# A first norm taken token by token on ScalarE, and the first two projections by chunk pairs

## The chip, the cores and the metric

The kernel runs on one core of one Trainium2 chip. The metric is the device time of one execution in microseconds. Five engines work side by side and meet only at semaphores: TensorE (PE; its weight loads are shown as PEld), VectorE (DVE), ScalarE (ACT), GpSimd (POOL) and SyncE (SP), which issues the DMAs.

## The reference, cut to what matters

Two transformer blocks over 512 tokens of width 1024, in float32. The first thing that is computed is a root-mean-square norm of x and the input projection:

```python
def rms_norm(x, g, eps=NORM_EPS):
    x32 = x.astype(jnp.float32)
    y = x32 * lax.rsqrt(jnp.mean(x32 * x32, axis=-1, keepdims=True) + eps)
    return (y * g.astype(jnp.float32)).astype(x.dtype)

h = rms_norm(x, norm_mix_pre_g[l])
proj = h @ w_in[l]
mq, mk, mv, dq, dk, dv, ga, gb = jnp.split(proj, split_at, axis=-1)
```

All that follows (two kinds of attention, gates, output projections, feed-forward parts, a second block with a recurrent mixer, stick-breaking attention and a memory) is the same in both kernels.

## The kernel before, in words

Activations are kept transposed: the width lies on partitions in 8 chunks of 128, the 512 tokens along the free axis. A matmul in full precision is made of three: each weight tile (128 output columns, 8 chunks, 512 KB in DRAM, buffer RAW) is split by `split` into a high part WH (ACT, L1178) and a rest WL (DVE, L1402); each activation chunk X is multiplied by the norm's gain and split into HH (ACT, L1184) and HL (DVE, L1412) by `feed`. `mm` (L971) then issues, for one chunk k and each weight of its group, WH with HH, WL with HH and WH with HL into one PSUM bank: 24 matmuls for a weight.

The norm's factor R per token is not applied before the projections but to their results: `normed` (L1431) multiplies the PSUM bank by R. So matmuls can begin before R is known.

A planner (`Plan`) writes one list of steps; each engine's program walks through that list in order and carries out the steps that it has a part in. The order of the list is therefore the order on every engine, and an engine that waits holds back all that stands behind it. Events are semaphores: `hi`/`lo` for a weight's parts, `xh`/`xl` for a chunk's, `mm` for the end of a projection.

The start of the kernel:

- SP issues the loads: chunk pairs of x (`load_x`, L1829, 512 KB each, tokens on partitions) and the first four weights in turn: x0, w0, x2, w1, x4, w2, x6, w3, then 17 small loads (`small_loads`), then further weights. Weight n goes into one of 4 RAW buffers and waits for the WL of weight n - 4.
- `turn_x` (L950): four 128x128 transposes on TensorE per chunk, into a bank; DVE copies it to X (L1407).
- `turns` (L474) is a generator: for chunk c it emits the transposes and the copy, then the `feed` of chunk c - 1, for c = 0 and 1 also the split of a weight. Three of its steps run before the first projection, the rest one by one in front of each `mm` step. So transposes stand two or three chunks ahead of the matmuls of the first group, q and k of head pair 0, which take both weights chunk by chunk.
- The sum of squares: `feed` calls `square`. ACT squares X per chunk (L1189), POOL adds to an accumulator (L1762), DVE adds the last (L1419), TensorE multiplies it by `onesD` (every element 1/1024, L1005), which gives the mean square of each token on all partitions, and `rstd` makes R of it: a table load (L115), Ln (L1197) and Exp (L1199) on ACT and three 128x512 operations on DVE (L1425, L1427, L1429).

After the group, `split_to` has ACT and DVE split weights 3 and 4 (counted from 0; they wait for the end of the first and second weight's matmuls, whose buffers they take), then come the steps of the norm, and then the third weight, vr.

## Time and profile before

| | us |
|---|---|
| median of 3 runs | 1995.89 |
| lowest, highest | 1995.13, 1997.08 |
| the profiled execution | 1994.75 |
| its span, first to last instruction | 1992.7 |

The page of the profile: PE busy 1962.3 us (98% of the span), PEld 1591.4, DVE 979.6, ACT 760.2, POOL 247.3; mean DMA rate 88 GB/s; mean granted clock of TensorE 0.997 of full speed. Busy times of single matmuls overlap, since they are pipelined; the time that one takes up is the distance from its start to the next one's. Times in the rows are microseconds from the start of the span; "xN" is a number of instructions merged into a row, and what stands in brackets is the idle time of the engine before the row and what ended it.

### The profile page before, as it was taken

Reading aid. Unit: us, or ns where it says so; the run is one execution under the profiler, and the core shown is the slowest. Engines: PE = TensorE matmul, PEld = TensorE weight load, DVE = VectorE, ACT = ScalarE, POOL = GpSimd, SP = SyncE. Lnnn points to the kernel's source line nnn. Section 1 sums busy time; section 2 is a strip of 40 time slices with the busy share of each in tenths; the row PEclk is TensorE's granted clock in tenths of the full one; section 3 lists DMA queues with packets and bytes.
Section 4 is the critical chain, followed back from the end, with each engine's and each line's share of the span. In section 5 each row is a group of like instructions: output and inputs, shape, how many; then the busy total and the mean of one; then the engine's idle time right before and its main releaser. Section 6 shows DMA issues by size and latency. Waiting matters only on the chain.

```text
span 1992.7 us, 22832 instructions
## 1 busy us (share of the span) xinstructions
PE 1962.3 (98%) x9092; PEld 1591.4 (80%) x9092; DVE 979.6 (49%) x1508; ACT 760.2 (38%) x1150; POOL 247.3 (12%) x253
## 2 busy tenths in 40 slices
PE   8999999999999999999999999999999999999997
PEld 6777788878888887788888878877887788888886
DVE  6677534373334335533433465675654454333334
ACT  5344523453232234422322355565543343222233
POOL 5221001201011011110100130122010011011012
PEclk9999999999999999999999999999999999999998
DMA  5212223433333324333333231211231233333322
GB/s 162 85 53 64 64 85 95 117 97 103 98 95 95 96 82 119 90 100 95 96 95 96 89 91 55 64 53 53 85 95 53 85 96 95 95 97 102 98 80 58
DMA packets 343402, 175.71 MB, mean 88 GB/s; under 512 B 6305, under 2 KB 343298, under 8 KB 343298
## 3 DMA queue, kind: packets, MB, share of 16 engines
q1 hardware_dynamic: 343298, 174.27, 30.1%
q8 instruction: 72, 1.18, 0.2%
q14 instruction: 32, 0.26, 0.0%
HBM read 172.15 MB, written 2.10 MB: 87 GB/s over the span
## 4 chain that ended last, share of the span: by engine, by line
PE 89%; DVE 7%; ACT 2%; issue 1%; DMA 0%; SPq 0%; POOL 0%; DVEq 0%; ACTq 0%
PE ps L982 27%; PE ps L986 27%; PE ps L984 27%; DVE WL L1402 1%; PE ps L1022 1%; PE ps L1042 1%; PE ps L1059 1%; PE ps L1120 1%; PE ps L995 1%; PE ps L1138 1%; PE ps L1012 1%; DVE TS L1435 1%; PE ps L1051 1%; DVE TS L1599 1%; PE ps L1063 1%
## 5 line engine op out<-in xcount | busy, mean ns | idle before, releaser
L1402 DVE TENSOR_TENSOR WL<-RAW,WH 128x1024 fp32r<-128x1024 f32 (+2 forms) x336 | 400.9, 1196 | 707.6 <-ACT WH L1178 707.3
L982 PE MATMUL ps<-HH,WH 128*128 128x512 f32 x1728 | 688.0, 398 | 0.0
L986 PE MATMUL ps<-HL,WH 128*128 128x512 f32 x1728 | 674.4, 390 | 2.0 <-DVE HL L1412 1.9
L984 PE MATMUL ps<-HH,WL 128*128 128x512 f32 x1728 | 673.6, 390 | 1.0 <-DVE WL L1402 1.0
L1178 ACT ACTIVATE WH<-RAW 128x1024 fp32r<-128x1024 f32 (+2 forms) x336 | 342.2, 1021 | 546.4 <-PE ps L986 538.1
L982 PEld LDWEIGHTS ps<-HH,WH 128*128 128x128 f32 x1728 | 324.7, 188 | 76.1 <-issue 8.8
L986 PEld LDWEIGHTS ps<-HL,WH 128*128 128x128 f32 x1728 | 324.6, 188 | 73.8 <-DVE HL L1412 5.6
L984 PEld LDWEIGHTS ps<-HH,WL 128*128 128x128 f32 x1728 | 324.8, 188 | 72.7 <-issue 5.3
L982 PE MATMUL ps<-GH,WH 128*128 128x512 f32 x720 | 282.0, 392 | 0.0
L986 PE MATMUL ps<-GL,WH 128*128 128x512 f32 x720 | 280.6, 390 | 0.0
L984 PE MATMUL ps<-GH,WL 128*128 128x512 f32 x720 | 280.2, 389 | 0.0
L1781 POOL TENSOR_TENSOR TS<-TS 128x512 f32<-128x512 f32 x66 | 85.1, 1290 | 936.4 <-ACT TS L1206 936.4
L986 PEld LDWEIGHTS ps<-GL,WH 128*128 128x128 f32 x720 | 135.1, 188 | 29.5 <-DVE GL L1441 1.3
L982 PEld LDWEIGHTS ps<-GH,WH 128*128 128x128 f32 x720 | 135.2, 188 | 28.8 <-ACT GH L1221 0.8
L984 PEld LDWEIGHTS ps<-GH,WL 128*128 128x128 f32 x720 | 135.2, 188 | 28.3 <-issue 0.5
L1206 ACT ACTIVATE TS<-TS 128x512 f32<-128x512 f32 x90 | 56.9, 632 | 212.4 <-DVE TS L1435 212.4
L1435 DVE SCALAR_TENSOR_TENSOR TS<-ps,TS 128x512 f32<-128x512 f32 x142 | 97.2, 686 | 81.2 <-PE ps L986 80.5
L1221 ACT ACTIVATE GH<-TS 128x512 fp32r<-128x512 f32 x78 | 49.3, 632 | 180.8 <-DVE TS L1532 125.0
L1762 POOL TENSOR_TENSOR TS<-TS 128x512 f32<-128x512 f32 (+1 forms) x48 | 60.4, 1258 | 374.6 <-ACT TS L1189 374.4
L1441 DVE TENSOR_TENSOR GL<-TS,GH 128x512 fp32r<-128x512 f32 x78 | 54.0, 692 | 54.5 <-ACT GH L1221 54.5
L1184 ACT ACTIVATE HH<-X,G 128x512 fp32r<-128x512 f32 x48 | 34.7, 723 | 64.0 <-DVE X L1557 44.5
L1412 DVE SCALAR_TENSOR_TENSOR HL<-X,G,HH 128x512 fp32r<-128x512 f32 x48 | 39.4, 822 | 19.3 <-ACT HH L1184 19.0
(197 smaller groups left out, 1509.1 us busy)
## 6 DMA issues: line engine op xcount, KB each, us to landing
RAW<-in_ffn_w_gu SPq DMA_DIRECT2D x88, 512.0 KB, 3.8
RAW<-in_w_in SPq DMA_DIRECT2D x68, 512.0 KB, 3.9
RAW<-in_ffn_w_down SPq DMA_DIRECT2D x32, 512.0 KB, 4.1
RAW<-in_w_gate SPq DMA_DIRECT2D x22, 512.0 KB, 3.7
RAW<-in_w_up SPq DMA_DIRECT2D x22, 512.0 KB, 3.9
RAW<-in_w_out SPq DMA_DIRECT2D x16, 512.0 KB, 4.1
RAW<-in_mem_w_kv SPq DMA_DIRECT2D x16, 512.0 KB, 3.9
RAW<-in_w_down SPq DMA_DIRECT2D x16, 512.0 KB, 4.1
```

The lines of the kernel that those rows point to most:

```text
L982: e.matmul(bk, wh, xh, start=k == 0, stop=False)
L984: e.matmul(bk, wl, xh, start=False, stop=False)
L986: last = e.matmul(bk, wh, xl, start=False, stop=k == kt - 1)
L1178: e.activation(m["WH"][:, s, 0:kt, :], m["RAW"][:, n % NRAW, 0:kt, :], ACT.Copy).then_inc(*sg.inc("hi", n))
L1206: e.activation(t, t, ACT.Silu if func == "Silu" else ACT.Sigmoid).then_inc(*sg.inc("fn", key))
L1221: e.activation(m[buf + "H"][:, n, :], at.view(src), ACT.Copy).then_inc(*sg.inc("xh", (buf, gen, n)))
L1402: e.tensor_tensor(m["WL"][:, s, 0:kt, :], m["RAW"][:, n % NRAW, 0:kt, :], m["WH"][:, s, 0:kt, :].bitcast(F32), ALU.subtract).then_inc(*sg. ...
L1412: e.scalar_tensor_tensor(m["HL"][:, c, :], X[:, c, :], G[:, gcol:gcol + 1], m["HH"][:, c, :].bitcast(F32), ALU.mult, ALU.subtract).then_in ...
L1435: e.scalar_tensor_tensor(at.tile(key), at.bank(bank), scale, at.tile(("R", R)), ALU.mult, ALU.mult).then_inc(*sg.inc("pj", key))
L1441: e.tensor_tensor(m[buf + "L"][:, n, :], at.view(src), m[buf + "H"][:, n, :].bitcast(F32), ALU.subtract).then_inc(*sg.inc("xl", (buf, gen, ...
L1762: e.tensor_tensor(a, a, s, ALU.add).then_inc(*sg.inc("acc", (acc, c)))
L1781: e.tensor_tensor(t, t, at.tile(("R", R)), ALU.mult).then_inc(*sg.inc("gr", key))
```

## The change

It does the following.

- The loads of x4 and x6 go ahead of the third and fourth weight.
- The first two projections are emitted by `first_pair`: for each pair of chunks c, c+1, the transposes and copies of both, the feeds of both, for c = 0 and 2 the split of one weight, the squares of the pair, then matmul steps of that pair for one weight (`which`), then for the other. At c = 0 only the first weight is taken; at c = 2 the second takes k = 0 to 3. After the last pair come the splits of weights 2, 3 and 4.
- The squares are taken on ACT from x as it was loaded (tokens on partitions): per pair four 128x256 activations with an accumulated sum along the row, into the 16 columns of XS. POOL's and DVE's adds of this norm are gone.
- `first_norm` replaces `rstd` for this norm: DVE sums XS to four values per partition and scales them, ACT takes Ln and Exp of 128x4 values, DVE refines them in three 128x4 operations and scales the identity four times into `diag`; TensorE multiplies `onesD` by `diag`, which spreads the four columns over all partitions, and DVE copies the bank to R.
- The scratch for dynamic DMA is 2048 in place of 4096; two small buffers are added.

```diff
+    def turn_pair(self, c):
+        for a in range(2):
+            self.bank(("tx", c + a))
+            self.step("turn_x", c + a)
+            self.banks.give(("tx", c + a), ("x", (0, c + a)))
+        for a in range(2):
+            self.step("feed", 0, c + a, c + a, ())
...
+    def first_pair(self, ps):
+
+        banks = [self.bank(("pb", key)) for key, *_ in ps]
+        self.weights += [(name, 0, KD, c0) for _, name, c0, *_ in ps]
+        self.groups.append((0, 2, ("H", 0, 0), banks, T, KD))
+        for c in range(0, KD, 2):
+            self.turn_pair(c)
+            if c < 4:
+                self.step("split", c // 2)
+            self.square_pair(c)
+            for i in range(2):
+                if (c, i) == (0, 1):
+                    continue
+                for k in range(0 if (c, i) == (2, 1) else c, c + 2):
+                    self.step("mm", 0, k, (i,))
+        self.n_split = 2
+        self.split_to(2 + NSPL)
+        return [self.normed(0, p[0], b, ("mm", i), *p[3:]) for i, (p, b) in enumerate(zip(ps, banks))]
...
@@ run
-            if self.total:
+            if self.total and c < 4:
                 self.dma()
+        for _ in range(2 if self.total else 0):
+            self.dma()
         self.tiles.take("small")
         self.step("small_loads")
-        turn = self.turns()
-        for _ in range(EARLY):
-            next(turn)
-        self.first_block(turn)
+        self.first_block()
...
@@ tensor_program
+    def first_norm(key):
+        g.wait_ge(*sg.at("ones", 0))
+        g.wait_ge(*sg.at("diag", 0))
+        wait_all(at.bank_free(("stat", key)))
+        e.matmul(at.bank(("stat", key)), m["onesD"], at.tile("diag"), start=True, stop=True).then_inc(*sg.inc("stat", key))
...
@@ scalar_program
+    def square_x(c):
+        v = at.x_pair(c)
+        g.wait_ge(*sg.at(f"d_x{c}", c))
+        for j in range(4):
+            h = slice(j % 2 * 256, j % 2 * 256 + 256)
+            wait_all(at.tile_free(("xq", c, j // 2)))
+            o = e.activation(at.tile(("xq", c, j // 2))[:, h], v[:, j, :], ACT.Square, accum_out=m["XS"][:, 4 * j + c // 2:4 * j + c // 2 + 1])
+        o.then_inc(*sg.inc("xq", c))
+
+    def first_norm(key):
+        N = m["XN"]
+        explog()
+        g.wait_ge(*sg.at("xm", 0))
+        g.wait_ge(*sg.at("ones", 0))
+        e.activation(N[:, 4:8], N[:, 0:4], ACT.Ln, bias=m["eps"][:, 0:1], scale=4.0).then_inc(*sg.inc("rs"))
+        g.wait_ge(*sg.last("rs"))
+        e.activation(N[:, 4:8], N[:, 4:8], ACT.Exp, scale=-0.5).then_inc(*sg.inc("rs", key))
...
@@ vector_program
+    def first_norm(key):
+        N, d = m["XN"], at.tile("diag").rearrange("p (i f) -> p i f", f=P)
+        for c in range(0, KD, 2):
+            g.wait_ge(*sg.at("xq", c))
+        e.tensor_reduce(N[:, 8:12], m["XS"].rearrange("p (i c) -> p i c", c=4), AX.X, ALU.add).then_inc(*sg.inc("xn"))
+        g.wait_ge(*sg.last("xn"))
+        e.tensor_scalar(N[:, 0:4], N[:, 8:12], 1.0 / D, None, ALU.mult).then_inc(*sg.inc("xm", 0))
+        g.wait_ge(*sg.at("rs", key))
+        e.scalar_tensor_tensor(N[:, 8:12], N[:, 4:8], 4.0, N[:, 4:8], ALU.mult, ALU.mult).then_inc(*sg.inc("xn"))
+        g.wait_ge(*sg.at("xm", 0))
+        g.wait_ge(*sg.last("xn"))
+        e.scalar_tensor_tensor(N[:, 8:12], N[:, 0:4], 1e-6, N[:, 8:12], ALU.add, ALU.mult).then_inc(*sg.inc("xn"))
+        g.wait_ge(*sg.last("xn"))
+        e.scalar_tensor_tensor(N[:, 4:8], N[:, 8:12], 3.0, N[:, 4:8], ALU.subtract, ALU.mult, reverse0=True).then_inc(*sg.inc("xn"))
+        g.wait_ge(*sg.last("xn"))
+        g.wait_ge(*sg.at("ident", 0))
+        wait_all(at.tile_free("diag"))
+        for j in range(4):
+            o = e.tensor_scalar(d[:, j, :], m["ident"], N[:, 4 + j:5 + j], float(D), ALU.mult, ALU.mult)
+        o.then_inc(*sg.inc("diag", 0))
+        g.wait_ge(*sg.at("stat", key))
+        wait_all(at.tile_free(("R", key)))
+        e.tensor_copy(at.tile(("R", key)), at.bank(("stat", key))).then_inc(*sg.inc("R", key))
...
-    nc = _bacc.Bacc("TRN2", target_bir_lowering=False, num_devices=1, dynamic_dma_scratch_size=4096)
+    nc = _bacc.Bacc("TRN2", target_bir_lowering=False, num_devices=1, dynamic_dma_scratch_size=2048)
```

## Rows read from the trace of the kernel before

**Rows 1.** The page: busy times, and the chain that ended last by engine.

```profile
PE 1962.3 (98%) x9092; PEld 1591.4 (80%) x9092; DVE 979.6 (49%) x1508; ACT 760.2 (38%) x1150; POOL 247.3 (12%) x253
PE 89%; DVE 7%; ACT 2%; issue 1%; DMA 0%; SPq 0%; POOL 0%; DVEq 0%; ACTq 0%
```

**Rows 2.** The timeline of TensorE, 9 to 29 us.

```profile
9.47 1.97 PE L958 MATMUL ps<-ident,TS 128*128 128x128 f32 x8 [2.89 <-DMA TS<-in_x]
...
12.09 0.63 PE L986 MATMUL ps<-HL,WH 128*128 128x512 f32 x1
12.51 0.63 PE L982 MATMUL ps<-HH,WH 128*128 128x512 f32 x1
...
18.66 0.50 PE L986 MATMUL ps<-HL,WH 128*128 128x512 f32 x1 [1.21 <-DVE HL L1412]
...
28.42 0.39 PE L986 MATMUL ps<-HL,WH 128*128 128x512 f32 x1
```

**Rows 3.** The chain that ended last, in order of time, 19 to 30 us: start, length.

```profile
19.85 0.44 PE ps L958 x4
...
28.81 0.86 PE ps L1005 x2
29.67 0.23 PE ps L982
```

**Rows 4.** Busy time by stretch, TensorE: stretch, length, busy, granted clock, DMA share, GB/s.

```profile
29.70:60.00 30.30, 30.30 (x140) 1.00 0.30 88
```

**Rows 5.** Who waited for whom, 0 to 40 us: total, times, longest.

```profile
PEld ps L986 <- DVE HL L1412: 3.6, 5, 1.6
```

**Rows 6.** The instructions that write HL, 0 to 30 us.

```profile
L1412 DVE SCALAR_TENSOR_TENSOR HL<-X,G,HH x8: 741/1257/1494, 10.7 to 26.1; 128x512 fp32r<-128x512 f32 x8
```

**Rows 7.** Busy time by stretch: PE, PEld, DVE, ACT, POOL, granted clock, DMA share, GB/s.

```profile
16.00:17.00 1.00, 1.00 (x8) 0.87 (x7) 1.00 (x2) 0.70 (x2) 0.22 (x1) 1.00 0.16 46
```

**Rows 8.** The timeline of ScalarE and VectorE, 7 to 11 us.

```profile
7.88 1.06 ACT L1178 ACTIVATE WH<-RAW 128x1024 fp32r<-128x1024 f32 x1 [5.82 <-DMA RAW<-in_w_in]
8.84 0.71 ACT L1184 ACTIVATE HH<-X,G 128x512 fp32r<-128x512 f32 x1
...
8.97 1.23 DVE L1402 TENSOR_TENSOR WL<-RAW,WH 128x1024 fp32r<-128x1024 f32 x1 [2.52 <-ACT WH L1178]
...
10.11 0.68 DVE L1407 COPY X<-ps 128x512 f32<-128x512 f32 x1
10.71 0.74 DVE L1412 SCALAR_TENSOR_TENSOR HL<-X,G,HH 128x512 fp32r<-128x512 f32 x1
```

**Rows 9.** The timeline of ScalarE, 1501 to 1503 us: activations with an accumulated sum.

```profile
1501.69 0.47 ACT L1308 ACTIVATE L<-ps,ST 128x256 f32<-128x256 f32 x1 [6.86 <-DVE ST L1653]
...
1502.15 0.47 ACT L1308 ACTIVATE L<-ps,ST 128x256 f32<-128x256 f32 x1
```

**Rows 10.** The timeline of ScalarE, 28 to 32 us.

```profile
30.25 1.28 ACT L115 ACT_TABLE_LOAD   x1
31.55 0.69 ACT L1197 ACTIVATE TS<-ps,eps 128x512 f32<-128x512 f32 x1
```

**Rows 11.** The timeline of ScalarE and VectorE at the last norm, 1981 to 1983 us.

```profile
1981.61 0.26 ACT L1321 ACTIVATE ST<-ps,eps 128x4 f32<-128x4 f32 x1 [2.40 <-PE ps L1146]
...
1982.15 0.16 DVE L1674 SCALAR_TENSOR_TENSOR ST<-ST 128x4 f32<-128x4 f32 x1 [2.21 <-ACT ST L1323]
```

**Rows 12.** Groups of VectorE instructions by shape, whole span: busy us, mean ns, idle before.

```profile
L1485 DVE TENSOR_SCALAR L<-L,ST 128x128 f32<-128x128 f32 x12 | 3.8, 316 | 0.0
```

**Rows 13.** Busy time by stretch near the end; columns as in rows 7.

```profile
1975.00:1980.00 5.00, 3.07 (x17) 2.35 (x15) 1.87 (x3) 1.11 (x2) 1.03 (x1) 1.00 0.00 0
1980.00:1982.00 2.00, 2.00 (x11) 2.00 (x12) 0.00 (x0) 0.35 (x2) 0.00 (x0) 0.58 0.00 0
```

**Rows 14.** The timeline of GpSimd and VectorE, 36 to 38.4 us.

```profile
36.28 2.07 POOL L1711 TENSOR_SCALAR_AFFINE_SELECT masks<-masks 128x128 f32<-128x128 f32 x3
...
36.98 1.22 DVE L1402 TENSOR_TENSOR WL<-RAW,WH 128x1024 fp32r<-128x1024 f32 x1
```

More of the change, by code:

```diff
@@ L27 @@
 NEG = -1.0e30
-EARLY = 3
 SUMMED = (1, 2)
@@ L208, in norm @@
             self.held[gen] = True
+            if gen == 0:
+                self.first_norm()
+                return ("n", 0)
             self.rstd(("n", gen), None if gen in SUMMED else ("n", gen), ("acc_last", ("n", gen)), "onesD", 0)
@@ L470, in out_proj, with square_pair, first_norm @@
         self.gfree = (mm,)
-    def turns(self):
-        for c in range(KD):
-            self.bank(("tx", c))
-            self.step("turn_x", c)
-            if c % 2:
-                self.tiles.give(("x", c - 1), ("tx", c))
-                self.tiles.give(("x", c), ("tx", c))
-            self.banks.give(("tx", c), ("x", (0, c)))
-            if c:
-                self.feed(0, c - 1, 0, ())
-            if c < 2:
-                self.split_to(self.n_split + 1)
-            yield
-        self.feed(0, c, 0, ())
+    def turn_pair(self, c):
[5 more added lines that the diff above has]
+            self.step("feed", 0, c + a, c + a, ())
+    def square_pair(self, c):
+        for a in range(2):
+            self.tiles.take(("xq", c, a))
+        self.step("square_x", c)
+        for a in range(2):
+            self.tiles.give(("xq", c, a), ("xq", c))
+        for a in range(2):
+            self.tiles.give(("x", c + a), ("tx", c + 1), ("xq", c))
+    def first_pair(self, ps):
[15 more added lines that the diff above has]
+        return [self.normed(0, p[0], b, ("mm", i), *p[3:]) for i, (p, b) in enumerate(zip(ps, banks))]
+    def first_norm(self):
+        key = ("n", 0)
+        self.bank(("stat", key))
+        self.tiles.take("diag")
+        self.tiles.take(("R", key))
+        self.step("first_norm", key)
+        self.tiles.give("diag", ("stat", key))
+        self.banks.give(("stat", key), ("R", key))
     def memory_in(self):
@@ L549, in project @@
                 if u == 0 and i == 0:
-                    return self.hgroup(0, ps[0:2], lambda: next(turn, None))
+                    return self.first_pair(ps[0:2])
                 if u == 0:
@@ L885, in view, with x_pair @@
         return self.bank(src[0])[:, src[1] * 256:(src[1] + 1) * 256]
+    def x_pair(self, c):
+        i = self.plan.tiles.slot["x", c]
+        return self.mem["TS"][:, i:i + 2, :].rearrange("p a t -> p (a t)").rearrange("p (i f) -> p i f", f=2 * P)
     def tile_free(self, key):
@@ L950, in turn_x @@
     def turn_x(c):
-        i = plan.tiles.slot["x", c // 2 * 2]
-        v = m["TS"][:, i:i + 2, :].rearrange("p a t -> p (a t)").rearrange("p (i f) -> p i f", f=2 * P)
-        bk, f = at.bank(("tx", c)), (c % 2) * P
+        v, bk, f = at.x_pair(c // 2 * 2), at.bank(("tx", c)), (c % 2) * P
         g.wait_ge(*sg.at("ident", 0))
@@ L969, in memory_turn, with mm @@
         i.then_inc(*sg.inc("mt", c))
-    def mm(gid, k):
+    def mm(gid, k, which=None):
         n, cnt, xs, banks, cols, kt = plan.groups[gid]
         xh, xl = at.x_hi(xs, k, cols), at.x_lo(xs, k, cols)
-        for i in range(cnt):
+        for i in which or range(cnt):
             s = (n + i) % NSPL
@@ L1335, in store @@
             o.then_inc(*sg.inc("oa", c))
-    todo = dict(split=split, feed=feed, square=square, rstd=rstd, normed=normed, plain=plain, turn=turn, split_tile=split_tile,
+    todo = dict(split=split, feed=feed, square=square, square_x=square_x, first_norm=first_norm, rstd=rstd, normed=normed,
+                plain=plain, turn=turn, split_tile=split_tile,
                 memory_hi=memory_hi, small_terms=small_terms, exps=exps, turn_probs=turn_probs, stick_map=stick_map,
```

13 lines of the change are left out of this document (7 added, 6 removed).

## The prediction

> **What bounds the kernel now.** I read the page first, then the waits of the first 40 us, and then the front of the kernel engine by engine. The page says that TensorE is busy for 98% of the span and carries 89% of the chain that ended last [rows 1]. So whatever the change does elsewhere is worth nothing unless it moves the moment at which TensorE can start a given matmul. All edits lie before the third weight, so there is one number to follow: when does TensorE begin with the third weight (the vr projection)? In the kernel before it issues the last matmul of the first two projections at 28.42, leaves it at 28.65, and spends 0.86 on the one matmul with onesD [rows 2, 3]. So the third weight begins at 29.5. From 29.7 to 60 TensorE is busy for 30.30 of 30.30 us [rows 4], so a delay at 29.5 is a delay of the end.
>
> In the front TensorE's weight loads wait on the HL split (3.6 us in 5 waits) [rows 5]. Transposes run two or three chunks ahead of the matmuls that need them, so the order costs nothing; what TensorE waits for is DVE's pace. HL takes 741 ns alone and 1257 to 1494 ns when POOL adds squares beside it [rows 6]. At 16 us the DMA engines fall idle (share 0.16): all eight 512 KB loads have landed [rows 7].
>
> **The change, part by part.** Times are us from the span's start. An engine takes its next instruction a little before the last record ends, so I use pitches from start to start: copy 0.60 (10.11 to 10.71) and WL 1.14 (8.97 to 10.11), HH 0.62 by its record of 0.71 less the same 0.1, WH 0.96 (7.88 to 8.84) [rows 8]. A warm group of four transposes is 0.44, a warm 128x512 matmul 0.23 [rows 3]; cold it is 0.42 (12.09 to 12.51), and eight transposes are 1.97 [rows 2].
>
> _Removed:_ seven POOL/DVE adds, eight 128x512 squares, three 128x512 DVE operations for R. This relieves POOL and DVE: eight HL at 0.74 instead of 1.26 give DVE back 4.2 us. It is a gain only where DVE is what TensorE waits for.
>
> _The first pair._ Transposes of chunks 0 and 1 end at 6.6 as before, HH0 and HH1 end by 8.1, WH0 (its data is there at 7.88) runs 8.1 to 9.1, WL0 to 10.4. TensorE issues one matmul at 9.2, five from 10.4 at 0.42: done at 12.5. Only now, since it works in order, come the transposes of chunks 2 and 3, which before ran at 9.47 [rows 2]: cold, to 14.5. Copies, HH2 and HH3 follow to 15.7, and WH1 stands behind them on ACT: 15.7 to 16.7, WL1 to 17.9. The first weight's k=2, 3 are done at 16.9, and eleven of the second weight's twelve matmuls go from 18.0 to 20.5.
>
> _The other two pairs._ Nothing of a pair is transposed ahead. Call T the start of its transposes. First bank out T+0.44, copies T+0.6 to T+1.9, HH T+1.33 and T+1.95 (end T+2.67), first matmul T+2.09, HL ends at T+2.83 and T+3.50, and the last of the twelve matmuls leaves at T+5.14. Work in that is 0.88 of transposes and 12 x 0.228 = 2.74; 1.5 is a round trip that nothing covers. So T is 20.5, then 25.6, and the projections end at 30.7 instead of 28.65: +2.1.
>
> _The squares._ Four 128x256 squares with an accumulated sum per pair; the nearest rows, exponentials of that size with accumulation, stand 0.46 apart [rows 9]. So 1.84 per pair on ACT. In the first three pairs it is hidden: the squares end at T+4.41, and ACT is next needed at T+5.14+1.33. In the last they are not hidden: behind them stand three weight splits, and behind those the norm.
>
> _The norm._ This is the largest term. TensorE's matmul with the diagonal stands before the third weight in its order, and it waits for a chain that begins behind work on ACT and DVE. ACT: HH7's slot ends T+2.57, squares T+4.41, WH2 T+5.37, WH3 T+6.33 (its wait for the first weight's matmuls is over), WH4 ends T+7.39 (waits for the second's, over too), table load 1.28 [rows 10] to T+8.7. DVE: WL2 begins T+5.5, WL3 T+6.6, WL4 T+7.8, ending at T+9.0. Then reduce and mean, 0.2 each; Ln and Exp 0.3 each with their hop; three 128x4 operations at 0.2 (0.26 and 0.16 long [rows 11]); four 128x128 scalings of the identity, 0.25 apart, the last 0.32 long [rows 12]. Diagonal ready T+11.6, the matmul 0.86, third weight at T+12.5 = 38.1. TensorE idles 6.5 us, from T+5.1 to T+11.65. Before, this matmul waited for nothing, because the R chain stood behind it. R itself comes earlier relative to the third weight (one 0.69 copy), but q and k are not read by TensorE until two weights later, so nothing is earned. Bounds: small operations between 0.15 and 0.32 each move this by -1.0 to +0.6.
>
> The sum so far: 38.1 - 29.5 = +8.6.
>
> _The clock._ At the end of the trace TensorE pauses 1.93 us in 1975 to 1980, and the next stretch shows a granted clock of 0.58 [rows 13]. After 6.5 idle us I expect 1.2 GHz again. In the front matmuls were still 0.42 apart at 12.51 [rows 2], some 3 us after TensorE had become busy at 9.47; at half speed for 3 to 4 us the loss is 1.5 to 2. I take +1.6 (ends 0 and +2.3). The front itself may stay at 1.2 GHz longer, since its activity is thinner: 0 to +4, and I take 0, because before a wait of 1.21 us at 18.66 [rows 2] was followed by matmuls 0.23 apart.
>
> _Rules of the Trainium skill against rows._ While TensorE waits, POOL fills masks (they move up, its adds gone). In the trace a WL of 1.22 runs at 36.98 beside such selects at 36.28, no slower than alone [rows 14]. The Trainium skill (GPSIMD Engine Reference, section Specifications) says that POOL shares SBUF interfaces with VectorE and contends with instructions of two SBUF inputs or a two-port mode. By that rule WL2 to WL4 and the scalings would stretch, and going by HL's ratio of rows 6 the wait would be some 2 to 3 us longer; by the row it is not. Second, the table load: the next Ln starts 0.02 after it [rows 10]. The Trainium skill (ScalarE: Activation LUTs, What ACT_TABLE_LOAD costs) adds a drain of about 1.38 us to the load, an estimate by which Ln would start 0.7 later; the rows show none, and the sum goes by them.
>
> _Hidden or free._ x4 and x6 go ahead of the third and fourth weight on SP; these land by 16 to 18, first read by ACT at 30. x6, needed at 25.6, comes no later than before. small_loads stay behind all eight; the fifth and sixth weight wait behind them until 18.3 either way, and WL1 is done by then. DMAs of weights 6 to 8 now wait on SP for WL2 to WL4 (32 and later), with the memory loads behind; weight 6 is read four weights, 22 us, after 38. The scratch of 2048 touches nothing that the issues in the trace use. All of this: 0; if SP had a stall, four weights of cover go first.
>
> **Total** +10.2. The profiled execution took 1994.75 (span 1992.7), 1.14 under the median of 1995.89. From the median: 2006.0.
>
> **Rivals.**
> 1. _The front stays cold._ Thin activity keeps 1.2 GHz through the second pair: 18 matmuls and eight transposes at double pitch, up to +4: 2010. For it: the clock rose late before, too. Against: the wait at 18.66 did not lower it.
> 2. _The pairs keep TensorE fed, only the norm's wait stays._ From WL0 at 10.4, 48 matmuls and six groups of transposes are 10.9 + 2.6: 23.9; with the norm's 6.5 + 0.9 the third weight begins at 31.3, +1.8: 1998, within no change. For it: DVE has 4 us more. Against: the order on TensorE, which has no transpose ahead of matmuls.
> 3. _Faster._ As 2, and the diagonal is ready when TensorE gets to it: 24.8, so -4.7: 1991. Its place is the first read of the diagonal on TensorE; it decides if ACT and DVE finish the norm by 24, that is if splits 2 to 4 and the squares are done some 6 us earlier than I work out. Two of those splits wait for the very matmuls that end at 24, which speaks against it.
>
> That the change does not do what it says I give no chance of its own: the steps in the diff fix the order on each engine, which runs its own list from front to back.
>
> **Chances.** Forecast (+6.5 to +12) 0.66; rival 1 0.14; rival 2 0.14; rival 3 0.06. About 0.2% (4 us) is what a measurement of this kernel can tell from no change. So slower 0.80, same 0.14, faster 0.06. The range: the forecast's own low end is +8.6, less 1.0 for the small operations and 1.0 for a pair that goes better than worked out: +6.6, or 2002.5; between it and rival 2's 1998 I put the lower end at 2000. Above, +10.2, 0.6 and 0.7 for the clock, and rival 1 at 2010 with as much again: 2012. That leaves out rival 3 and most of rival 2, nearly 0.2.
>
> **What would show it.** In the changed profile: the transposes of chunk 2 after six matmuls, about 12.5; three of the four pairs with a wait of TensorE on the HH or HL of its own chunk; the last projection matmul near 30.7; then one idle stretch of 6 to 7 us released by DVE's diagonal, the third weight near 38, and matmuls 0.42 apart just after. Wrong if that idle stretch is under 4 us, if the last projection matmul leaves before 28, or if the third weight's start is late by 8 us and the end is not.

## The result, and the profile after

The kernel after takes 2006.33 us (median of 4 runs, 2006.02 to 2006.78), the kernel before 1995.51 beside it (4 runs, 1994.3 to 1997.08): +10.8 us, ratio 1.0053 with a 95% interval of 1.004 to 1.0065. The forecast was 2006.0 with a range of 2000 to 2012. The profiled execution of after took 2006.78, its span 2005.0.

The page answers to [rows 1]: the same 9092 matmuls, DVE and POOL a little less busy, ACT a little more.

```profile
span 2005.0 us, 22855 instructions
...
PE 1966.6 (98%) x9092; PEld 1593.3 (79%) x9092; DVE 976.3 (49%) x1514; ACT 761.5 (38%) x1174; POOL 237.3 (12%) x247
```

TensorE's busy time grew by only 4.3 us while the span grew by 12.3; the rest is idle time. The timeline of TensorE in the kernel after, 8 to 44 us, shows where (L992 transposes, L1016, L1018 and L1020 the projections' matmuls, L1036 the norm's):

```profile
12.84 1.91 PE L992 MATMUL ps<-ident,TS 128*128 128x128 f32 x8
15.43 0.50 PE L1016 MATMUL ps<-HH,WH 128*128 128x512 f32 x1 [0.68 <-ACT HH L1224]
...
18.50 0.50 PE L1018 MATMUL ps<-HH,WL 128*128 128x512 f32 x1 [0.69 <-DVE WL L1461]
...
21.18 1.04 PE L992 MATMUL ps<-ident,TS 128*128 128x128 f32 x8
23.31 0.50 PE L1016 MATMUL ps<-HH,WH 128*128 128x512 f32 x1 [1.10 <-ACT HH L1224]
...
26.56 1.04 PE L992 MATMUL ps<-ident,TS 128*128 128x128 f32 x8
28.70 0.50 PE L1016 MATMUL ps<-HH,WH 128*128 128x512 f32 x1 [1.10 <-ACT HH L1224]
...
32.02 0.39 PE L1020 MATMUL ps<-HL,WH 128*128 128x512 f32 x1
37.86 2.05 PE L1036 MATMUL ps<-TS,onesD 128*128 128x512 f32 x2 [5.45 <-issue]
38.91 1.42 PE L1016 MATMUL ps<-HH,WH 128*128 128x512 f32 x1
40.13 0.63 PE L1018 MATMUL ps<-HH,WL 128*128 128x512 f32 x1
40.55 0.63 PE L1020 MATMUL ps<-HL,WH 128*128 128x512 f32 x1
```

After each of the three later groups of eight transposes TensorE waits for the HH of its own chunk (0.68, 1.10, 1.10); after the last pair it waits 5.45 us for the diagonal; and just behind that, matmuls are 0.42 apart (40.13 to 40.55). The profile names no releaser for the 5.45 us ("issue"). That it is the diagonal follows from the times (the last scaling on DVE ends at 37.76, the matmul starts at 37.86) and from e5_warm below, whose row names it.

Against [rows 2]: the last projection matmul issues at 32.02 where it issued at 28.42. The norm's matmul starts at 37.86; in the kernel before (timeline of TensorE) it started at 28.65 and waited for nothing:

```profile
28.65 1.02 PE L1005 MATMUL ps<-TS,onesD 128*128 128x512 f32 x2
```

By the chain that ended last, it takes 2.05 us in the kernel after, where it took 0.86, and the third weight begins at 39.90, where it began at 29.67 [rows 3]:

```profile
37.86 2.05 PE ps L1036 x2
39.90 0.43 PE ps L1016
```

The timelines of ScalarE and VectorE in the kernel after show what the diagonal waited for: the squares, three splits, then the small operations. The table load ends at 35.00, before DVE's mean is there, and Ln is released by that mean: the load is beside the chain and not in it.

```profile
29.17 0.40 ACT L1232 ACTIVATE TS<-TS 128x256 f32<-128x256 f32 x1
...
29.57 0.40 ACT L1232 ACTIVATE TS<-TS 128x256 f32<-128x256 f32 x1
...
30.76 2.94 ACT L1218 ACTIVATE WH<-RAW 128x1024 fp32r<-128x1024 f32 x3
33.72 1.28 ACT L114 ACT_TABLE_LOAD   x1
35.66 0.30 ACT L1240 ACTIVATE XN<-XN,eps 128x4 f32<-128x4 f32 x1 [0.65 <-DVE XN L1480]
```

```profile
31.84 3.50 DVE L1461 TENSOR_TENSOR WL<-RAW,WH 128x1024 fp32r<-128x1024 f32 x3 [1.36 <-ACT WH L1218]
...
36.88 0.88 DVE L1492 TENSOR_SCALAR TS<-ident,XN 128x128 f32<-128x128 f32 x4
```

And the stretches of the kernel after, with the columns of [rows 7], show the granted clock falling in the pause and staying at 0.50, which is the 1.2 GHz level, until 42 us; [rows 4] had 1.00 throughout.

```profile
34.00:36.00 2.00, 0.00 (x0) 0.00 (x0) 1.59 (x4) 1.32 (x3) 0.00 (x0) 0.80 0.84 237
36.00:38.00 2.00, 0.14 (x1) 0.17 (x2) 1.36 (x7) 0.19 (x1) 0.00 (x0) 0.50 0.96 277
...
40.00:42.00 2.00, 2.00 (x6) 1.52 (x6) 1.90 (x3) 0.00 (x0) 0.00 (x0) 0.50 0.04 12
42.00:44.00 2.00, 2.00 (x10) 1.61 (x9) 0.02 (x1) 0.00 (x0) 0.00 (x0) 1.00 0.04 8
```

**One landmark for all kernels.** The times of single executions of one kernel differ by up to 4 us (one cause comes below). For the account I therefore use the start of the first attention scores, the first matmuls after the front that every version has in the same place. They begin at 40.52 in the kernel before and at 51.81 in the kernel after (the timeline of TensorE, first of before, then of after):

```profile
40.52 1.77 PE L1022 MATMUL ps<-TS 64*128 64x512 f32 x8
```

```profile
51.81 1.77 PE L1062 MATMUL ps<-TS 64*128 64x512 f32 x8
```

That is +11.29, beside +10.8 in the medians. It divides without a rest: the last projection matmul leaves at 32.25 (32.02 + 0.23) instead of 28.65, **+3.60**; from there to the norm's matmul at 37.86, **+5.61**; and from the start of the norm's matmul to the scores 13.95 instead of 11.87 us for the same work, **+2.08**, the low clock.

**A second place where the clock can fall.** Some 75 us behind the landmark every profiled execution comes to two short waits of TensorE among attention scores, 0.62 and 0.82 us long in the kernel before, 0.62 to 0.64 and 0.82 in all others. In the kernel before the clock stays at 1.00 there; in e3_both it does not. The stretch 116 to 124 us, first of before, then of e3_both, with the columns of [rows 7]:

```profile
116.00:124.00 8.00, 7.07 (x27) 5.01 (x28) 7.04 (x18) 1.58 (x2) 0.72 (x1) 1.00 0.23 66
```

```profile
116.00:124.00 8.00, 7.18 (x17) 4.93 (x17) 6.68 (x17) 1.58 (x2) 0.00 (x0) 0.57 0.22 66
```

From the landmark to the end of the span the profiled executions without such a fall (before, e1_ahead, e5_warm, e6b_old_loads, e10_small) take 1951.6 to 1952.2 us; those with one take 1953.2 to 1953.8 (after, e2_late, e4_norm_before_splits, e6_old_order, e8_loads, e9_best) or 1955.2 and 1955.3 (e3_both, e7_old_norm). The work and the waits there are the same, so no edit of the front explains it. It is also the best account that the record has of the spread within one kernel: of the 23 runs of the kernel before beside e1_ahead, the 14 with a mean granted clock of 0.996 took 1995.19 to 1997.47, the nine with 0.997 or 0.998 took 1993.67 to 1994.89. Where landmark and median disagree by 1 us or so, the landmark is the better measure of the front.

### The profile page after: what moved, and what is told of

The parts are those of the page before. It is cut to its first block, busy times and chain, and to the rows that moved or that the text cites. A ratio compares the mean times of both kernels' runs of the same rounds, so it can differ in the third digit from the quotient of the medians.

```text
span 2005.0 us, 22855 instructions
## 1 busy us (share of the span) xinstructions
PE 1966.6 (98%) x9092; PEld 1593.3 (79%) x9092; DVE 976.3 (49%) x1514; ACT 761.5 (38%) x1174; POOL 237.3 (12%) x247
## 4 chain that ended last, share of the span: by engine, by line
PE 89%; DVE 7%; ACT 2%; issue 1%; POOL 0%; DMA 0%; DVEq 0%; SPq 0%; ACTq 0%
PE ps L1016 27%; PE ps L1020 27%; PE ps L1018 27%; DVE WL L1461 1%; PE ps L1062 1%; PE ps L1082 1%; PE ps L1099 1%; PE ps L1160 1%; PE ps L1029 1%; PE ps L1178 1%; PE ps L1052 1%; DVE TS L1518 1%; PE ps L1091 1%; DVE TS L1682 1%; PE ps L1103 1%
## 5 line engine op out<-in xcount | busy, mean ns | idle before, releaser
L1016 PE MATMUL ps<-HH,WH 128*128 128x512 f32 x1728 | 689.6, 399 | 5.4 <-ACT HH L1224 2.9
L1018 PE MATMUL ps<-HH,WL 128*128 128x512 f32 x1728 | 674.9, 391 | 1.8 <-DVE WL L1461 1.8
L1020 PE MATMUL ps<-HL,WH 128*128 128x512 f32 x1728 | 675.5, 391 | 0.7 <-DVE HL L1471 0.6
L1016 PEld LDWEIGHTS ps<-HH,WH 128*128 128x128 f32 x1728 | 325.4, 188 | 83.5 <-issue 9.0
L1018 PEld LDWEIGHTS ps<-HH,WL 128*128 128x128 f32 x1728 | 325.5, 188 | 74.1 <-issue 5.6
L1020 PEld LDWEIGHTS ps<-HL,WH 128*128 128x128 f32 x1728 | 325.3, 188 | 72.7 <-DVE HL L1471 4.6
L1016 PE MATMUL ps<-GH,WH 128*128 128x512 f32 x720 | 282.1, 392 | 0.0
L1020 PE MATMUL ps<-GL,WH 128*128 128x512 f32 x720 | 280.6, 390 | 0.0
L1018 PE MATMUL ps<-GH,WL 128*128 128x512 f32 x720 | 280.2, 389 | 0.0
L1020 PEld LDWEIGHTS ps<-GL,WH 128*128 128x128 f32 x720 | 135.2, 188 | 29.5 <-DVE GL L1524 1.3
L1016 PEld LDWEIGHTS ps<-GH,WH 128*128 128x128 f32 x720 | 135.2, 188 | 28.8 <-ACT GH L1279 0.8
L1018 PEld LDWEIGHTS ps<-GH,WL 128*128 128x128 f32 x720 | 135.2, 188 | 28.1 <-issue 0.5
L1846 POOL TENSOR_TENSOR TS<-TS 128x512 f32<-128x512 f32 (+1 forms) x42 | 52.7, 1254 | 358.4 <-ACT TS L1247 358.1
L1224 ACT ACTIVATE HH<-X,G 128x512 fp32r<-128x512 f32 x48 | 34.5, 723 | 73.4 <-DVE X L1640 44.5
L1615 DVE TENSOR_TENSOR TS<-ps,TS 128x512 f32<-128x512 f32 x66 | 45.2, 684 | 6.4 <-POOL TS L1865 6.4
```

The costliest lines, as they stand in the source:

```text
L1016: e.matmul(bk, wh, xh, start=k == 0, stop=False)
L1018: e.matmul(bk, wl, xh, start=False, stop=False)
L1020: last = e.matmul(bk, wh, xl, start=False, stop=k == kt - 1)
L1615: e.tensor_tensor(t, at.bank(bank), t, ALU.mult).then_inc(*sg.inc("gu", key))
L1846: e.tensor_tensor(a, a, s, ALU.add).then_inc(*sg.inc("acc", (acc, c)))
```

## The experiments

Theory: three things make the loss, each separately removable. (a) Within a pair nothing is transposed ahead, so TensorE waits for a round trip. (b) The norm's matmul stands before the third weight and waits for a chain that ACT and DVE begin only behind three splits. (c) That wait lowers the clock. Rivals: the loads' new order or DMA waits; the new norm's own cost; the order of the squares. The last has no experiment of its own: in the kernel after, the squares take 1.59 us of ACT ahead of the splits (29.17 to 30.76), which is part of (b). All kernels were edited from the kernel after, and line numbers move by a few lines from one to the next. Gathered here, since every reading below uses it ("+" is against the kernel before, measured beside it; the scores' start is that of one profiled execution):

| kernel | longest wait near the norm's matmul | scores start | medians (before) | change | ratio, 95% |
|---|---|---|---|---|---|
| before | none | 40.52 | 1995.51 | | |
| after | 5.45 | 51.81 | 2006.33 | +10.8 | 1.0053, 1.004 to 1.0065 |
| e1_ahead | 7.60 | 46.65 | 2000.64 (1995.44) | +5.2 | 1.0028, 1.0018 to 1.0038 |
| e2_late | 0.48 | 44.82 | 1998.98 (1995.44) | +3.5 | 1.0018, 1.0009 to 1.0028 |
| e3_both | 1.71 | 39.55 | 1995.66 (1995.44) | +0.2 | 1.0001, 0.9991 to 1.0011 |
| e5_warm | 0.87 | 49.45 | 2003.86 (1995.44) | +8.4 | 1.0045, 1.003 to 1.006 |
| e4_norm_before_splits | 3.17 | 49.41 | 2004.09 (1995.24) | +8.9 | 1.0043, 1.0029 to 1.0056 |
| e6_old_order | 5.63 | 49.22 | 2003.73 (1995.24) | +8.5 | 1.0041, 1.0027 to 1.0055 |
| e6b_old_loads | 6.15 | 47.08 | 2001.47 (1995.02) | +6.4 | 1.0032, 1.002 to 1.0043 |
| e8_loads | 5.52 | 51.21 | 2006.50 (1995.02) | +11.5 | 1.0055, 1.004 to 1.007 |
| e7_old_norm | none | 49.90 | 2006.07 (1995.24) | +10.8 | 1.0054, 1.004 to 1.0068 |
| e9_best | none | 36.77 | 1991.84 (1995.24) | -3.4 | 0.9981, 0.9972 to 0.999 |
| e10_small | 0.1 | 38.34 | 1991.74 (1995.02) | -3.3 | 0.9984, 0.9975 to 0.9993 |

Scores' start and median agree within 1.5 us in every row. So the front, up to the scores, explains the large differences; the rest is of the size of the late fall of the clock.

### The transposes a pair ahead (e1_ahead)

```diff
+        self.turn_pair(0)
         for c in range(0, KD, 2):
-            self.turn_pair(c)
             if c < 4:
                 self.step("split", c // 2)
             self.square_pair(c)
+            if c + 2 < KD:
+                self.turn_pair(c + 2)
```

> The changed kernel with each pair's transposes emitted ahead of the matmuls of the pair before. Theory (the front lost time because TensorE, working in order, does no transposes ahead, so each pair pays a round trip through DVE and ACT): the last projection matmul leaves near 25.5 instead of 32.25, the wait for the diagonal stays at 5 to 6 us, the third weight starts some 6.5 us earlier, the time is about 2000. Rival (the pace of ACT and DVE bounds the front, the order on TensorE does not matter): the last projection matmul stays within 1 us of 32, the time within 1 us of the changed kernel's 2006.3.

Measured +5.2 instead of +10.8. The timeline of TensorE in e1_ahead:

```profile
24.59 0.39 PE L1022 MATMUL ps<-HL,WH 128*128 128x512 f32 x1
32.58 2.05 PE L1038 MATMUL ps<-TS,onesD 128*128 128x512 f32 x2 [7.60 <-issue]
```

From 11 to 25 us TensorE is busy for 13.98 of 14.00 us: with the transposes ahead, (a) is gone, and the last projection matmul issues 7.4 us earlier than in after. But of those 7.4 the wait takes 2.15 back (7.60 for 5.45). The rest arrives at the landmark: 5.2 of 7.4. I had expected the wait to stay at 5 to 6 us; the timeline of ScalarE in e1_ahead shows what lengthened it. The split of the fifth weight, ahead of the norm, waited 2.14 us for its load, which costs no wait in the kernel after:

```profile
26.92 1.06 ACT L1220 ACTIVATE WH<-RAW 128x1024 fp32r<-128x1024 f32 x1 [2.14 <-DMA RAW<-in_w_in]
```

### The norm's matmul behind the third weight (e2_late)

```diff
-        return [self.normed(0, p[0], b, ("mm", i), *p[3:]) for i, (p, b) in enumerate(zip(ps, banks))]
+        self.first_done = [(p, b, ("mm", i)) for i, (p, b) in enumerate(zip(ps, banks))]
+        return None
+
+    def third(self, ps):
+        b = self.bank(("pb", ps[0][0]))
+        mm, = self.mtiles([(ps[0][1], 0, KD, ps[0][2])], ("H", 0, 0), [b], ahead=False)
+        self.norm(0)
+        return [self.normed(0, p[0], b, mm, *p[3:]) for p, b, mm in self.first_done + [(ps[0], b, mm)]]
```

> The changed kernel with the norm's matmul (and the scaling of q and k by R) emitted behind the third weight's matmuls. Theory (the 5.6 us idle stretch is TensorE waiting in order for the diagonal, and the low clock follows from it): no idle stretch over 1.5 us after the front, the diagonal is ready when the third weight ends near 38, granted clock 1.00 throughout, time about 1999 (7 us less than the changed kernel). Rival (the third weight would not be ready any earlier, since its WL stands behind the squares): third weight cannot start before 36, and less than 2 us are won.

Measured +3.5. In the timeline of TensorE in e2_late the long wait is gone; 0.48 for the third weight's WL is what is left of it, and the norm's matmul, behind 24 others, waits for nothing:

```profile
33.03 0.50 PE L1025 MATMUL ps<-HH,WL 128*128 128x512 f32 x1 [0.48 <-DVE WL L1468]
...
38.39 1.02 PE L1043 MATMUL ps<-TS,onesD 128*128 128x512 f32 x2
```

The granted clock is 1.00 from 20 to 60 us. At the landmark this gives 6.99: (b) and (c) together, 5.61 + 2.08 less the 0.48 and small change. What stays is (a) with that 0.48: 4.3 at the landmark, 3.5 in the medians.

### Both (e3_both)

The two edits together.

> Both edits: transposes a pair ahead, norm's matmul behind the third weight. Theory: the two losses are separate and add up; third weight starts near 25.6, and the time is 3 us under the kernel before: about 1992.5. Rival (losses overlap, or the norm's chain is then late for the matmul after the third weight): not below 1997.

At the landmark -12.26 against after, and the two alone were -5.16 and -6.99: they add up. Yet the median, expected at 1992.5, is only level with the kernel before (interval 0.9991 to 1.0011). Two things stand between. First, the landmark itself is only 0.97 earlier than the kernel before's, because one wait is left, 1.71 at the norm's matmul, and the timeline of ScalarE in e3_both says why:

```profile
27.49 1.06 ACT L1227 ACTIVATE WH<-RAW 128x1024 fp32r<-128x1024 f32 x1 [1.93 <-DMA RAW<-in_w_in]
```

The split of the fifth weight stands before the norm on ACT and waited 1.93 for its DMA, as in e1_ahead. With TensorE early, the norm's chain reached a load that had been hidden before. The pause of 1.71 did not lower the clock. Second, the profiled execution lost 3.0 us behind the landmark to the late fall of the clock shown above (1955.2 for 1952.2). How often the other runs have it is not on record; their mean granted clock, 0.995 or 0.996 in nine of ten, is on the low side of the kernel before's.

### The pause filled with matmuls (e5_warm)

```diff
+        wait_all(at.bank_free(("stat", key)))
+        g.wait_ge(*sg.at("hi", 2))
+        for i in range(20):
+            e.matmul(at.bank(("stat", key)), m["WH"][:, 2, i % KD, :], m["HH"][:, i % KD, :], start=True, stop=True)
         g.wait_ge(*sg.at("diag", 0))
-        wait_all(at.bank_free(("stat", key)))
```

The 20 matmuls write into the bank that the norm's matmul then overwrites.

> The changed kernel, TensorE given 20 matmuls of 128x512 whose results nobody reads, into the norm's bank, ahead of its wait for the diagonal; about 4.6 us of work inside the 5.6 us wait. Theory (the pause lowers the granted clock, and that costs 2.1 us after the wait): the norm's matmul starts at 37.9 as before, the clock stays at 1.00, the norm's matmul takes 0.86 and the next ones are 0.23 apart: 2.1 us less, about 2004.2. Rival (the low clock costs nothing that counts, or another pause sets it): the clock drops all the same, and the time is within 0.5 us of the changed kernel.

The timeline of TensorE in e5_warm:

```profile
31.91 4.70 PE L1037 MATMUL ps<-HH,WH 128*128 128x512 f32 x20
37.47 1.13 PE L1039 MATMUL ps<-TS,onesD 128*128 128x512 f32 x2 [0.87 <-DVE TS L1495]
```

The clock stays at 1.00, and the scores begin 2.36 earlier. 0.39 of that is the norm's matmul starting earlier; from its start to the scores it is 11.98 instead of 13.95, so (c) is 1.97 by this run and 2.08 by the account above. The medians move by 2.4.

### The norm before two of the splits (e4_norm_before_splits)

```diff
         self.n_split = 2
+        self.split_to(3)
+        self.norm(0)
         self.split_to(2 + NSPL)
```

> The changed kernel with the steps of the norm emitted between the split of weight 2 and the splits of weights 3 and 4; the norm's matmul still stands before the third weight. Theory (two of the three splits stand in the chain that TensorE waits for): WL3 and WL4 leave the chain, the diagonal is ready 2.4 us earlier, TensorE idles 3.2 us instead of 5.6, and 2.4 us are won if the granted clock falls all the same, 4.4 if it stays: 2003.9 or 2001.9. Rival (the squares and the small operations make the wait, not the splits): under 1 us won.

The timeline of TensorE in e4_norm_before_splits:

```profile
32.26 0.40 PE L1022 MATMUL ps<-HL,WH 128*128 128x512 f32 x1
35.83 1.67 PE L1038 MATMUL ps<-TS,onesD 128*128 128x512 f32 x2 [3.17 <-issue]
```

Two splits (0.98 apart on ACT, 1.14 on DVE) moved behind the norm take 2.28 off the wait, 2.40 off the landmark and 2.0 off the median. So the splits ahead of it are part of (b), as theory has it, but not most of it: the rest is the squares, one split and the small operations. The table load is again not in the chain: Ln starts 0.28 after its end, when DVE's mean is there. Nor does a wait of 3.17 spare the clock: 36 to 40 us is granted 0.57.

### The order of the kernel before, with the new norm (e6_old_order, e6b_old_loads)

```diff
+    def turns(self):
+        for c in range(KD):
+            self.bank(("tx", c))
+            self.step("turn_x", c)
+            self.banks.give(("tx", c), ("x", (0, c)))
+            if c:
+                self.step("feed", 0, c - 1, c - 1, ())
+            if c % 2:
+                self.square_pair(c - 1)
+            if c < 2:
+                self.split_to(self.n_split + 1)
+            yield
+        self.step("feed", 0, c, c, ())
...
     def first_pair(self, ps):
+        turn = self.turn0
+        return self.hgroup(0, ps, lambda: next(turn, None))
```

e6b_old_loads has the old order of the loads as well.

> The order of the front of the kernel before (transposes two or three chunks ahead, both weights chunk by chunk), with the loads and the new norm of the change: the norm alone. Theory (pair order and norm lose separately; DVE's relief is real and was hidden by the pair order): the last projection matmul leaves before 26.5 (28.65 in the kernel before), the wait for the diagonal is 5 to 7.5 us with a fall of the clock after it, time about 2001. Rival (relief of DVE is worth nothing): it leaves after 28, time above 2003.

> The kernel of the run e6_old_order (order of the front as before, new norm) with the loads also in the old order. Its ACT stood 3.16 us, to 15.66, at the split of the third weight, with the feeds behind it; the kernel before stood there to 14.51. Theory (the third weight comes a transfer's share later because x4 and x6 went ahead of it, and in this order ACT is in need of it): that wait ends 1.1 us earlier, the last projection matmul leaves some 1 us earlier (28.4 instead of 29.5), time 1 us less, about 2002.7. Rival (the wait does not carry through to TensorE): the last projection matmul leaves at 29.5 as before.

With the new loads the front missed what I expected: the last projection matmul issues at 29.28, later than in the kernel before. The timeline of ScalarE in e6_old_order names the cause, that of TensorE the effect:

```profile
15.66 1.06 ACT L1239 ACTIVATE WH<-RAW 128x1024 fp32r<-128x1024 f32 x1 [3.16 <-DMA RAW<-in_w_in]
```

```profile
17.39 0.50 PE L1037 MATMUL ps<-HH,WH 128*128 128x512 f32 x1 [1.07 <-ACT HH L1245]
...
19.31 0.80 PE L1041 MATMUL ps<-HL,WH 128*128 128x512 f32 x1 [1.19 <-DVE HL L1492]
...
20.33 0.63 PE L1039 MATMUL ps<-HH,WL 128*128 128x512 f32 x1
20.76 0.63 PE L1041 MATMUL ps<-HL,WH 128*128 128x512 f32 x1
```

In this order the third weight's split stands on ACT before the feed of chunk 2, and with x4 ahead of that weight's load ACT stood there until 15.66. The clock was granted at 0.62 from 18 to 22 us. With the old loads (e6b_old_loads) the split starts at 14.17, a wait of 0.81 for WL and one of 0.81 for HL are left (13.61 and 17.88), the clock stays at 1.00, and the last projection matmul issues at 26.42, 2.0 before the kernel before's and 2.86 before e6_old_order's, where I had expected 1.1. That 2.0 is what the new norm gives the front: the eight HL take 736 to 798 ns here, where six of the kernel before's ran beside POOL's adds and took 1.19 to 1.49 us. It still ends at +6.4, because the wait for the diagonal is 6.15:

```profile
26.42 0.39 PE L1039 MATMUL ps<-HL,WH 128*128 128x512 f32 x1
32.97 2.04 PE L1055 MATMUL ps<-TS,onesD 128*128 128x512 f32 x2 [6.15 <-issue]
```

### The old order of the loads alone (e8_loads)

```diff
-            if self.total and c < 4:
+            if self.total:
                 self.dma()
-        for _ in range(2 if self.total else 0):
-            self.dma()
```

> The changed kernel with the loads in the order of the kernel before (x0, w0, x2, w1, x4, w2, x6, w3). Theory (the new order of the loads buys nothing here, since x4 and x6 are read only at 21.2 and 26.6): transposes of chunk 4 near 21.2 and of chunk 6 near 26.6 wait for no DMA, scores within 0.5 us of the changed kernel's 51.8, time within 1 us of 2006.3. Rival: a wait on x6 appears, more than 1 us lost.

+11.5 with an interval that contains after's +10.8, and scores 0.60 earlier: in the pair order the moved loads are worth nothing measurable. They matter only in an order that needs the third weight at 14 us.

### The pair order with the norm of the kernel before (e7_old_norm)

```diff
         for a in range(2):
-            self.step("feed", 0, c + a, c + a, ())
+            self.tiles.give(("x", c + a), ("tx", c + 1))
+        for a in range(2):
+            self.feed(0, c + a, 0, ())
...
-            self.square_pair(c)
...
-            if gen == 0:
-                self.first_norm()
-                return ("n", 0)
```

> The pair order of the change with the norm of the kernel before (squares per chunk on ACT, adds on POOL and DVE, no diagonal): the order alone. Theory: each of the later three pairs loses its round trip, longer by a square on ACT and by the slower HL beside POOL; the last projection matmul leaves near 34.5, nothing waits after it, the clock stays up; time about 2001.5. Rival (the pair order loses only together with the new squares): it leaves before 31, time under 1998.

The timeline of TensorE in e7_old_norm:

```profile
18.93 0.50 PE L1018 MATMUL ps<-HL,WH 128*128 128x512 f32 x1 [0.61 <-DVE HL L1469]
...
21.15 0.50 PE L1016 MATMUL ps<-HH,WL 128*128 128x512 f32 x1 [1.48 <-DVE WL L1459]
...
21.81 0.63 PE L1014 MATMUL ps<-HH,WH 128*128 128x512 f32 x1
22.23 0.63 PE L1016 MATMUL ps<-HH,WL 128*128 128x512 f32 x1
...
38.03 1.02 PE L1043 MATMUL ps<-TS,onesD 128*128 128x512 f32 x2
```

The norm's matmul waits for nothing, as in the kernel before. But the projections end at 38.03, not near 34.5 as I had expected: each of the later pairs waits, behind the 1.10 for its HH, again for HL, which DVE makes beside POOL's add (0.61), the second pair 1.48 more for a WL that took 2.06 us, and matmuls are 0.42 apart from 21.8 to 24.8. So the order alone costs 9.4 at the landmark with the old norm, but only 3.6 of front with the new one. The parts of the change are not terms that add: the new norm takes 5.8 of the order's damage out of the front and puts 7.7 back, as its wait and the low clock (5.61 + 2.08).

### What beats both kernels (e9_best, e10_small)

e9_best has the transposes ahead, the norm's ACT and DVE part between the third and the fourth weight's split as in e4, and the norm's matmul and the copy of R behind the third weight:

```diff
         self.n_split = 2
+        self.split_to(3)
+        self.norm(0)
         self.split_to(2 + NSPL)
...
+    def third(self, ps):
+        b = self.bank(("pb", ps[0][0]))
+        mm, = self.mtiles([(ps[0][1], 0, KD, ps[0][2])], ("H", 0, 0), [b], ahead=False)
+        self.first_stat()
+        return [self.normed(0, p[0], b, mm, *p[3:]) for p, b, mm in self.first_done + [(ps[0], b, mm)]]
```

e10_small is e3_both with the small loads issued behind those of the fifth and sixth weight.

> Transposes a pair ahead; the norm's part on ACT and DVE between the splits of weights 2 and 3, its matmul and the copy to R behind the third weight's matmuls. Theory: the remaining wait of 1.7 us at the norm's matmul, seen with both edits, was ACT waiting for the fifth weight's DMA ahead of the norm; it goes, TensorE has no wait from 11.5 to the first scores, which begin near 37.8 (40.5 before), and the time is 2.5 us under the kernel before, about 1993. Rival (something later takes the gain back): scores begin near 37.8, the time is within 1 us of the kernel before.

> The kernel of the run e3_both with the 17 small loads issued behind the fifth and sixth weight instead of ahead of them. There ACT waited 1.93 us, to 27.49, for the fifth weight's DMA, ahead of the norm. Theory (that DMA is held back by the small loads ahead of it on the queue): the fifth weight lands before 20, the wait is gone, and TensorE's wait at the norm's matmul shrinks from 1.7 us to under 1; scores near 38.8. Rival (the DMA waits for its buffer, freed by WL0 at 10.5, or for something else): it still lands near 27.

Both are faster than both kernels: 0.9981 (0.9972 to 0.999) and 0.9984 (0.9975 to 0.9993) of the kernel before. Busy time of TensorE by stretch in e9_best, columns as in [rows 7]:

```profile
11.00:30.00 19.00, 19.00 (x88) 15.47 (x88) 14.75 (x25) 14.61 (x37) 16.74 (x41) 1.00 0.66 175
30.00:60.00 30.00, 30.00 (x146) 22.80 (x144) 18.58 (x61) 13.09 (x28) 6.05 (x7) 1.00 0.31 88
```

There is no gap from 11 to 60 us, so this is what the new norm and the pairs with transposes ahead are worth together once the norm is hidden: 3.75 at the landmark. The load is 1.93 late in e3_both because of the 17 small loads ahead of it: SyncE issues them one by one from 11.92 to 20.4 us and the weight only at 20.42, and from 18 to 22 us the DMA engines are nearly idle. In e10_small the two weights are issued by 16.5, their bytes move before the small loads', and the wait of ACT for a DMA is gone, as is TensorE's of 1.71. By stretch, first e3_both, then e10_small:

```profile
18.00:22.00 4.00, 4.00 (x24) 3.37 (x23) 2.35 (x4) 2.53 (x9) 3.27 (x11) 1.00 0.09 23
...
24.00:27.00 3.00, 3.00 (x14) 2.33 (x13) 2.48 (x2) 1.55 (x2) 2.79 (x4) 1.00 0.92 267
```

```profile
18.00:22.00 4.00, 4.00 (x24) 3.39 (x23) 1.99 (x4) 2.17 (x8) 3.26 (x12) 1.00 0.50 142
```

## Why the prediction was right, and where its steps were off

**The mechanism and the place.** Each sign that it named is in the trace: eight transposes behind six matmuls (12.84 for 12.5), three pairs with a wait on their own HH, one idle stretch of 5.45 that ends with the diagonal, the norm's matmul at 37.86 for 37.25 (T+11.65 with T = 25.6), and matmuls 0.42 apart behind it. e1_ahead, e2_late, e3_both and e5_warm show by taking each away that these three are the loss.

**The front: +2.1 expected, +3.6 measured.** This is the term of the sum that was mis-sized. The round trip itself was right (first matmul at T+2.13, worked out as T+2.09). What I left out: the first matmuls behind a wait are 0.34 to 0.45 apart, not 0.23, and HL is again late by 0.2 to 0.3. Twelve matmuls then take 3.25 where I had 3.05; the last pair takes 3.55, its first HL being 0.96 long. With 0.34 lost in the cold first pair and 0.3 in the second, T was 21.18 and 26.56 for 20.5 and 25.6, and the end 32.25 for 30.7.

**The norm's wait: 6.5 expected, 5.61 measured** (from where the last projection matmul leaves; 5.45 is the idle time behind its record). Counted from T = 26.56, the chain on ACT and DVE came out 0.35 short: squares 0.40 apart and not 0.46 (they end T+4.20 for T+4.41), the table load ends T+8.44 for T+8.7, the scalings are 0.22 apart for 0.25, and the norm's matmul begins at T+11.30 for T+11.65. The rest is TensorE: its last projection matmul leaves at T+5.69 for T+5.14, and a chain that hangs on T does not move with that, so what this last pair loses more, the wait loses less. That is why two terms missed by +1.5 and -0.9, and the sum for the start of the norm's matmul, +9.21 for +8.6, by only 0.6. Of the 0.9 that cancelled, 0.55 is this structure; the 0.35 by which the chain was short is luck.

**The clock: +1.6 expected, +2.08 measured**, inside its bounds of 0 and 2.3. e4_norm_before_splits (1.7, from the norm's matmul to the scores 13.58 us where the kernel before takes 11.87), e1_ahead and e6b_old_loads (2.2 each) show that a pause of 3.17 costs nearly as much as one of 7.60. And e8_loads, with a pause of 5.52, paid 1.7 where the kernel after paid 2.08 for 5.45.

**Sum:** +11.3 at the landmark and +10.8 in the medians for +10.2. The forecast of 2006.0 is nearer to the measured 2006.33 than that, because it stood on a median of 1995.89 for the kernel before, which came out at 1995.51 beside the kernel after. Agreement to 0.3 us is luck; to 1 us it is the sum. The prediction also had no term for the late fall of the clock, which is 1.0 us of the profiled span's +12.3.

**The relief of DVE** by 4.2 us took the median of [rows 6], 1.257, for the time of all eight HL. Two of them took 0.74 and six 1.19 to 1.49, which makes 3.5. The sum does not use it.

**"Transposes stand ahead, so what TensorE waits for is DVE's pace"** was only half of what held the kernel before. e6_old_order and e6b_old_loads show that in its order a wait of ACT for the third weight's DMA stands before the feeds too, and the timeline of ScalarE in the kernel before has it:

```profile
14.51 1.06 ACT L1178 ACTIVATE WH<-RAW 128x1024 fp32r<-128x1024 f32 x1 [1.12 <-DMA RAW<-in_w_in]
```

For the forecast it made no difference, since the new order has no such split in the front. **The moved loads at 0** held (e8_loads), but in the old order the same edit costs 2.1 at the landmark, the fall of the clock at 19 us included.

**The rivals.** Rival 1, a cold front: did not occur, the second pair's matmuls are 0.23 apart once running; but e7_old_norm (0.70 from 20 to 24 us) and e6_old_order (0.62 from 18 to 22) had it in their fronts. Rival 2, pairs keep TensorE fed: excluded, by the order as argued; e1_ahead is that kernel, and at +5.2 it is dearer than the +1.8 I gave the rival, because with TensorE ahead the wait grows to 7.60, 2.14 of it for a load, and the clock falls. Rival 3, faster: no run has it as it stood, with the diagonal ready at 24. e9_best meets its condition, the diagonal ready when TensorE reaches it, another way, by moving the matmul, and gains 3.4 (3.75 at the landmark) of the 4.7 that I worked out.

**The two rules.** POOL finished its masks at 30.2 us, so nothing ran beside WL2 to WL4 (1.14 apart, the pitch of before) and the rule of the Trainium skill on shared interfaces (GPSIMD Engine Reference, section Specifications) was not put to the test there. Where the masks did run beside the chain, it held in part: a WL took 1.35 us in e1_ahead and 1.36 in e9_best, but 1.23 in e3_both as alone, and the four scalings 1.46 in e1_ahead and e3_both for 0.88. So the row of a WL of 1.22 beside such selects [rows 14] did not show the whole of it; in the kernel after that made no difference. After the table load Ln started 0.66 later, released by DVE's mean, and in e3_both and e9_best 0.40 and 0.42 later. So the drain of about 1.38 us that the Trainium skill names (ScalarE: Activation LUTs, What ACT_TABLE_LOAD costs) does not show in this kernel.

**Left open:** why fronts with waits of 1.1 to 1.5 us lost the clock in e6_old_order and e7_old_norm, and those with 1.10 in after and 1.71 in e3_both did not. Each front is known from one execution, and the two short waits behind the landmark show that the same work with the same waits keeps the clock in one execution and loses it in another. So the difference between those fronts need not lie in the kernels.

## What to carry to other kernels

Before a producer chain is moved, look at where its consumer stands on the busiest engine: a matmul emitted in its old place waits for the whole new chain, and moving just that matmul behind the next weight gave back 7 of 11 us without any faster instruction. Work that is grouped by chunk pairs needs the next group's first step emitted before this group's matmuls, or each group pays one full round trip. Cost such terms as a chain from a common start, not as independent additions: a last pair that ended later shortened the wait behind it by as much. When a front becomes earlier, ask which load it will now meet: in e1_ahead and e3_both that was the fifth weight's, and e10_small got it back by the order of the loads alone. And compare kernels at a landmark behind the change, in one view for both: the medians hold 1 to 3 us of a clock that falls elsewhere.

## What the runs showed of the hardware that I had not expected

- What POOL does decides how much DVE suffers. Beside masks (memset and affine select) HL took 752 to 954 ns in after; beside POOL's adds 1.19 to 1.49 us, 0.74 alone [rows 6]; in e7_old_norm a WL that began beside an add took 2.06 us for 1.23 [rows 8]. In e9_best, where DVE was busier, both sides slowed: four scalings took 1.15 us for 0.88 in after, and the three selects beside them 2.76 us for 1.02 in after at 19.65.
- 17 small loads issued in front of a weight hold it back by several us (their issue alone lasts from 11.92 to 20.4 us in e3_both), with the DMA engines nearly idle meanwhile: between 18 and 22 us the DMA engines moved 23 GB/s in e3_both and 142 in e10_small.
- A pause of 1.71 us left the clock at 1.00 (e3_both), one of 1.93 at the end of the kernel before did not [rows 13], and pauses of 3.17 to 7.60 all lowered it to the 1.2 GHz level. Their price, 1.7 to 2.2 us, hardly depended on their length. Waits of 0.63 and 0.82 kept it in some executions and lowered it in others, at a price of 1 to 3 us.
- An activation with an accumulated sum of 128x256 is followed by an accumulator read of 0.19 us, but that lies beside the next one: they stand 0.40 apart, the length of one record.
